# Rope keys in two groups of 64 columns, half of the expert combination as diagonal products, and another load order in the readout

## The chip, the cores and the metric

The kernel runs on one core of a Trainium2 chip. The core has five instruction streams: TensorE (PE in the rows; PEld is its weight load), VectorE (DVE), ScalarE (ACT), GpSimd (POOL) and SyncE (SP), which here only issues transfers. The metric is the device time of one execution in microseconds (us), taken as the median over runs. All arithmetic is in 32-bit floats.

## What is computed

The reference is a chain of three layers over 512 tokens x of 1024 features, with a context of 256 tokens: a gated-delta layer followed by a mixture of 64 experts, an RWKV layer, and a latent-attention (MLA) layer. Three places matter here. Cut to them:

```python
# 1. end of the first layer: six experts per token, weighted, then gate, add, norm
x = x + gt2 * moe_ffn(...)            # sum over the TOP_K = 6 chosen experts
x = rmsnorm(x, g_final)
# 2. readout of the RWKV layer, for all 768 tokens
yf = y[0] + jnp.flip(y[1], 1)
yn = ((yf - mean) * lax.rsqrt(var + GN_EPS)).reshape(B, T, D) * lnx_g + lnx_b
o = (yn + bonus.reshape(B, T, D)) * jax.nn.silu(gate)
d = o @ w_out                         # then x = x + g * d
# 3. inputs of the attention layer
p = h @ w_in
q_c, kv_c, k_pe, gate = jnp.split(p, [Q_LORA, Q_LORA + KV_LORA, Q_LORA + KV_LORA + QK_ROPE], axis=-1)
k_pe = concatenate([x1 * c - x2 * s, x1 * s + x2 * c])   # 32 rope features, x tokens only
```

## The kernel before, in words

The program is a row of phases. Each phase is a block with one instruction stream per engine, written out by hand and kept in that order; engines wait for each other through counted semaphores, and at a phase's end all engines meet at a barrier. Tokens lie in tiles of 128 (P): NT = 6 tiles, JC = 2 of context and JX = 4 of x. D = 1024, KD = 8 blocks of 128 features. Three phases are touched.

**combine** (span time about 1373 to 1431 us). The expert rows of x come back from memory as `rows[:, j, k, :]`, k = 0..5 of token tile j. SP asks for them in eight loads of 1.5 MB (`in0` to `in7`; `in(2j)` holds k = 0..2 of tile j and `in(2j+1)` k = 3..5), all on one queue, then for the context (`ctx_in`). DVE alone does the sum: six passes `acc = row * weight + acc` per tile (L2437), then the gate (L2440), the addition to the tokens (L2442) and, one tile behind, `norm(j-1)` (L2424, L2428). ACT takes the lengths (L2396, L2402) that norm needs, and at the end the squares that the next layer's norm needs; L2418 and L2447 close the phase. PE has no work in it.

**rwkv_readout** (about 2242 to 2381 us). For each of the six tiles j: DVE and ACT make the normed row `y` from two halves that the scan left in memory (`R.mean`, `R.centre`, `R.sum`, `R.finish`), POOL scales the bonus (`R.values`, L3114, L3117), PE turns it (`turn`, L3600), multiplies it with the output weights in two halves (`project`, L3610, 16 products each), and DVE adds the result to the tokens (`add`, L3706 and L3709). Tiles 0 and 1 are normed in the phase before. PE also works off one slice of the next layer's modulation weights per tile (`M.part`, L246; slices are 2 MB, `M.load`). The order on each engine is fixed:

```python
# PE, for j: project(j, 0), turn(j + 1), M.part(j), M.sum(j - 1), project(j, 1)
# DVE, for j: add(j, 0), copy_in(j + 1), norm(j + 2), add(j, 1)
```

`add(0, 0)` first waits for `x_in`, the landing of the tokens `K.X` (3 MB) and of the two gate rows `K.gate` (0.5 MB each). `R.load(sp, j)` is four loads of 0.5 MB (y, y2, bonus, gate) into one of two slots; R.load(j) may start when tile j-2 is turned.

**mla_inputs** (about 2392 to 2506 us). PE makes the latents (L3800, ten units), then the rope keys (L3806), then the gate (L3815, 64 products). The rope keys use a weight block of 96 columns, in which the 32 columns stand at 0 and at 64 (zeros elsewhere, set by POOL), and a second block with the halves exchanged: three passes over columns of `hT` (256 context tokens, 512 x tokens plain, 512 x tokens exchanged), 8 products each. DVE then copies and rotates (L3852 to L3857) and SP copies the result to further partitions.

Of the kernel before, what the change touches and what calls it, by code (L numbers as in the profile page):

```python
# [2363 lines left out]
def combine(K, I, acc, ys, w_of, spare, inv):  # L2364
# [6 lines left out]
    names = ("added gated ctx_in g_in sq_done rms_done v_step normed rms2_done " + " ".join(f"in{n}" for n in range(len(LOADS))))  # L2371
    with ExitStack() as c, phase(nc, names) as (block, S):
        buf = lambda name, shape: c.enter_context(sbuf(nc, name, shape, F32))
        gb, junk, st = buf("gain", [P, D]), buf("junk", [P, D]), buf("stats", [P, 5, NT])
        rows = spare[:, 0:JX * TOP_K * D].rearrange("p (j k n) -> p j k n", j=JX, k=TOP_K)

# [12 lines left out]
        def _(act):  # L2389
# [31 lines left out]
        def _(dve):  # L2421
# [9 lines left out]
            for j in range(JX):  # L2431
                for k in range(TOP_K):
                    if k % (TOP_K // 2) == 0:
                        dve.wait_ge(S[f"in{LOADS.index((j, k // (TOP_K // 2)))}"], 16)
                    if k:
                        dve.wait_ge(S["added"], j * TOP_K + k)
                    dve.scalar_tensor_tensor(out=acc[:, j, :], in0=rows[:, j, k, :], scalar=w_of[:, k, j:j + 1],  # L2437
                                             in1=acc[:, j, :], op0=ALU.mult, op1=ALU.add).then_inc(S["added"], 1)
                dve.wait_ge(S["added"], (j + 1) * TOP_K)
# [1104 lines left out]
def rwkv_readout(K, I, R, tokens, gate_rows):  # L3544
# [6 lines left out]
    with ExitStack() as c, phase(nc, names, R.S) as (block, S):  # L3551
# [219 lines left out]
def mla_inputs(K, I, qc, kvc, ssq, gT, kT, L, ws, pool_):  # L3771
# [4 lines left out]
    names = "rot lat_mm copied squared pe_mm rope1 w_zero pe_out doubled gate_mm gate_out"  # L3776
    with ExitStack() as c, phase(nc, names, L) as (block, S):
        wg, rest = gate_weights(pool_), pool_[:, 2 * KD * 512:]
        wr = rest[:, 0:2 * KD * QK].rearrange("p (a k n) -> p a k n", a=2, k=KD)
        t = rest[:, 2 * KD * QK:2 * KD * QK + 2 * TX].rearrange("p (a n) -> p a n", a=2)  # L3780
# [11 lines left out]
        def _(pe):  # L3792
# [41 lines left out]
        @block.gpsimd  # L3834
        def _(pool):
            pool.memset(wr[:, :, :, :], 0.0).then_inc(S["w_zero"], 1)

        @block.vector
        def _(dve):
            dve.wait_ge(S["w_in"], 16)  # L3840
            dve.wait_ge(S["w_zero"], 1)
# [517 lines left out]
```

## Time and profile before

| | |
|---|---|
| median of 3 runs | 2868.86 us (2866.93 to 2870.2) |
| the profiled execution | 2869.81 us, span 2868.0 us |
| instructions in it | 45580 |
| granted TensorE clock, mean | 0.931 of full speed |
| PE / PEld / DVE / ACT / POOL busy | 86% / 50% / 47% / 25% / 17% of the span |
| moved by DMA | 471.24 MB, mean 164 GB/s |

Busy shares are means over all phases; PE is busy most of the time but idle in some phases. What a change in one phase is worth has to be read from that phase. A matmul of 32-bit floats shows as two rows of the profile per product in the code (64 products at L3815 are 128 rows), so a count "x48" in a row is 24 products.

### The profile page before, as it was taken

Reading aid. Unit: us, or ns where it says so; the run is one execution under the profiler, and the core shown is the slowest. Engines: PE = TensorE matmul, PEld = TensorE weight load, DVE = VectorE, ACT = ScalarE, POOL = GpSimd, SP = SyncE. Lnnn points to the kernel's source line nnn. Section 1 sums busy time; section 2 is a strip of 40 time slices with the busy share of each in tenths; the row PEclk is TensorE's granted clock in tenths of the full one; section 3 lists DMA queues with packets and bytes.
Section 4 is the critical chain, followed back from the end, with each engine's and each line's share of the span. In section 5 each row is a group of like instructions: output and inputs, shape, how many; then the busy total and the mean of one; then the engine's idle time right before and its main releaser. Section 6 shows DMA issues by size and latency. Waiting matters only on the chain. (4 is left out here: it accounts for less than half of the span.)

```text
span 2868.0 us, 45580 instructions
## 1 busy us (share of the span) xinstructions
PE 2465.2 (86%) x18102; PEld 1445.2 (50%) x18102; DVE 1346.4 (47%) x2688; ACT 709.0 (25%) x1273; POOL 487.4 (17%) x474
## 2 busy tenths in 40 slices
PE   4999764987899999998079999979999599989998
PEld 2554354954444443343035557448887346455553
DVE  1550646533611111111678895976666561044442
ACT  3111440102211111111225561123333113044441
POOL 0000142300111111111000000033332230035550
PEclk7999776999899999999589999999999799999999
DMA  6110610014789999996525656334554832021001
GB/s 243 67 59 1 235 23 17 7 59 168 268 333 391 387 418 407 399 388 262 204 87 136 169 153 191 114 121 131 136 164 124 319 118 97 8 42 22 10 30 66
DMA packets 328951, 471.24 MB, mean 164 GB/s; under 512 B 151497, under 2 KB 225139, under 8 KB 304037
## 3 DMA queue, kind: packets, MB, share of 16 engines
q1 hardware_dynamic: 302677, 373.92, 37.9%
q10 hardware_dynamic: 12960, 69.21, 5.9%
q0 software_dynamic: 13104, 25.19, 2.3%
q8 instruction: 146, 2.39, 0.3%
q14 instruction: 64, 0.52, 0.1%
HBM read 413.82 MB, written 76.55 MB: 171 GB/s over the span
## 5 line engine op out<-in xcount | busy, mean ns | idle before, releaser
L1980 PE MATMUL psum<-ex_w,hT 128*64 128x512 f32 (+1 forms) x1104 | 330.6, 619 | 27.4 <-DMA ex_w<-in_exp_w_up 25.7
L1980 PEld LDWEIGHTS psum<-ex_w,hT 128*64 128x64 f32 (+1 forms) x1104 | 125.6, 159 | 226.7 <-issue 224.4
L4126 POOL TENSOR_SCALAR mla_pool<-mla_pool,at_stats 128x768 f32<-128x768 f32 x64 | 140.3, 2206 | 253.1 <-DVE at_stats L4144 253.1
L2212 DVE COPY slot_act_t<-psum 128x256 f32<-128x256 f32 x45 | 19.1, 424 | 327.0 <-PE psum L1988 327.0
L551 PE MATMUL psum<-hT,weights 128*128 128x512 f32 x384 | 166.8, 592 | 0.0
L1996 PE MATMUL psum<-ex_w,slot_act_t 128*64 128x512 f32 (+1 forms) x552 | 163.4, 597 | 1.4 <-DVE slot_act_t L2212 1.4
L1965 POOL DMA_INDIRECT scratch_ys<-slot_out,slot_row x45 | 45.4, 1008 | 468.2 <-issue 405.6
L551 PEld LDWEIGHTS psum<-hT,weights 128*128 128x128 f32 x384 | 73.0, 190 | 86.7 <-issue 86.1
L2168 ACT ACTIVATE slot_silu<-psum 128x256 f32<-128x256 f32 x45 | 17.3, 385 | 400.2 <-PE psum L1980 400.2
L3323 PE MATMUL psum<-rs_r_ident,rs_k_ident 64*64 64x96 f32 x1536 | 86.5, 252 | 15.3 <-POOL rs_k_ident L3295 14.0
L4024 PE MATMUL psum<-mla_kT,at_qT 128*128 128x512 f32 (+1 forms) x256 | 93.3, 489 | 2.6 <-DVE at_qT L4136 1.6
L1996 PEld LDWEIGHTS psum<-ex_w,slot_act_t 128*64 128x64 f32 (+1 forms) x552 | 55.8, 153 | 75.8 <-issue 71.2
L2715 PE MATMUL psum<-rh_lerp,rh_w 128*128 128x512 f32 (+1 forms) x256 | 91.1, 513 | 1.8 <-issue 1.8
L2219 DVE COPY slot_out<-psum 128x512 f32<-128x512 f32 x45 | 31.1, 692 | 128.9 <-PE psum L1996 128.9
L4149 DVE TENSOR_REDUCE at_stats<-psum 128x1 f32<-128x768 f32 x64 | 61.1, 955 | 61.8 <-PE psum L4024 61.6
L4099 ACT ACTIVATE mla_pool<-psum,at_stats 128x768 f32<-128x768 f32 x64 | 57.7, 902 | 127.5 <-DVE at_stats L4154 127.5
L2792 PE MATMUL psum<-rh_w,rh_lerp 128*128 128x256 f32 (+1 forms) x288 | 84.9, 457 | 0.0
L2679 PE MATMUL psum<-rh_lerp,rh_w 128*128 128x512 f32 (+1 forms) x256 | 83.9, 486 | 0.7 <-issue 0.7
L2792 PE MATMUL psum<-tokens,rh_lerp 128*128 128x512 f32 x192 | 82.7, 592 | 0.0
L3323 PEld LDWEIGHTS psum<-rs_r_ident,rs_k_ident 64*64 64x64 f32 x1536 | 67.7, 134 | 25.2 <-POOL rs_k_ident L3295 15.1
L3502 ACT ACTIVATE rs_w<-psum 128x256 f32<-128x256 f32 x96 | 36.9, 384 | 175.5 <-PE psum L3339 175.4
L3454 DVE TENSOR_TENSOR rs_right<-psum,rwkv_decay 64x512 f32<-64x512 f32 x94 | 64.6, 688 | 27.3 <-PE psum L3370 25.8
(612 smaller groups left out, 4731.0 us busy)
## 6 DMA issues: line engine op xcount, KB each, us to landing
ex_w<-in_exp_w_gate SPq DMA_DIRECT2D x64, 1024.0 KB, 9.1
ex_w<-in_exp_w_up SPq DMA_DIRECT2D x64, 1024.0 KB, 18.9
ex_w<-in_exp_w_down ACTq DMA_DIRECT2D x60, 1024.0 KB, 10.2
mod_ring<-in_w_mod SPq DMA_DIRECT2D x12, 2048.0 KB, 14.0
scratch_features<-tokens SPq DMA_DIRECT2D x96, 256.0 KB, 3.7
weights<-in_w_in SPq DMA_DIRECT2D x6, 2048.0 KB, 8.0
ex_w<-in_mod_w SPq DMA_DIRECT2D x6, 2048.0 KB, 12.5
ex_w<-scratch_ys SPq DMA_DIRECT2D x8, 1536.0 KB, 19.0
```

The lines of the kernel that those rows point to most:

```text
L551: mm = pe.matmul(K.bank[2 * (f % 4)][:, :], K.wring[:, n % RING, k, m * P:(m + 1) * P], K.hT[:, k, TC:TT], start=(k == 0), stop=(k == KD - 1))
L1980: mm = pe.matmul(bank[at:at + n, :], XT[:, k, at:at + n], W[:, 0:2, k * DE:(k + 1) * DE], start=(k == 0), stop=(k == KD - 1))
L1996: mm = pe.matmul(bank[at:at + n, :], aT[:, m, at:at + n], W[:, 2, m * D + h * 512:m * D + (h + 1) * 512], start=(m == 0), stop=(m == 1))
L2679: mm = pe.matmul(K.bank[b][:, 0:t1 - t0], rk_w(s)[:, 1, k, :], lerp[:, 0, k, t0:t1], start=(k == 0), stop=(k == KD - 1))
L2715: mm = pe.matmul(K.bank[2 + seg][:, 0:t1 - t0], rk_w(s)[:, 0, k, :], lerp[:, 1, k, t0:t1], start=(k == 0), stop=(k == KD - 1))
L2792: mm = pe.matmul(K.bank[u % 4][:, 0:cols], lerp[:, n, k, j * P:(j + 1) * P], w[:, k, :], start=(k == 0), stop=(k == KD - 1))
L3323: m = pe.matmul(K.bank[scb(u, k)[p]][kb_at[p], ch * P:ch * P + W], KI[part, k, ch, kb_at[p]], RI[part, k, ch, :], start=True, stop=True)
L3454: dve.tensor_tensor(RV[part, u % 2, ch, p::2, :], K.bank[SB][part, :].rearrange("p (k n) -> p k n", n=HD), Dg[part, d, :, at:at + 1].broad ...
L4024: mm = pe.matmul(K.bank[2 * (u % 2) + b][:, 0:t1 - t0], qT[:, s, h, qt * P:(qt + 1) * P], kT[:, s, h, t0:t1], start=True, stop=True)
L4099: act.activation(Pm[:, q % 2, u, :], K.psum[:, b * 512:b * 512 + TT], ACT.Exp, bias=st[:, 1, u:u + 1], scale=SCALE, accum_out=st[:, 2, u:u ...
L4126: pool.tensor_scalar(Pm[:, q % 2, u, :], Pm[:, q % 2, u, :], st[:, 3, u:u + 1], None, ALU.mult)\
L4149: dve.tensor_reduce(st[:, 0, u:u + 1], K.psum[:, b * 512:b * 512 + TT], AX.X, ALU.max)\
```

## The change

Three independent edits. In combine, tiles 1 to 3 sum only the expert rows k = 0..2 on DVE; rows k = 3..5 are summed by PE as products with diagonal matrices that hold the weights (made by ACT from the identity), two halves of 512 columns with three products each, into two PSUM banks, and DVE adds that with one pass. ACT takes the squares of the context after tile 2 and not at the end. In the readout SP asks for tile 2's four arrays right after the vectors, ahead of the first slice of modulation weights, the tokens and the gate rows; it waits first for the scan's stores and for `turned`. The third slice of modulation weights, and those after it, come later in SP's order. In mla_inputs the weight block has 64 columns (32 plain, 32 exchanged); two groups g multiply it with columns 0..383 and 384..767 of `hT`, and write partitions 0..63 and 64..127 of one PSUM bank. POOL's clearing of the block is gone, and DVE's rotation takes its inputs by group.

```diff
@@ combine: names and TensorE @@
-    names = ("added gated ctx_in g_in sq_done rms_done v_step normed rms2_done " + " ".join(f"in{n}" for n in range(len(LOADS))))
+    names = ("diag_set half_mm added gated ctx_in g_in sq_done rms_done v_step normed rms2_done " + " ".join(f"in{n}" for n in range(len(LOADS))))
...
+        HALF = TOP_K // 2
+        diag = buf("weight_diagonals", [P, JX - 1, HALF, P])
+        total = lambda j: K.psum[:, (j % 2) * 2 * 512:(j % 2 + 1) * 2 * 512]
+
+        @block.tensor
+        def _(pe):
+            for j in range(1, JX):
+                pe.wait_ge(S["diag_set"], HALF * j)
+                pe.wait_ge(S[f"in{LOADS.index((j, 1))}"], 16)
+                if j > 2:
+                    pe.wait_ge(S["added"], TOP_K + (j - 2) * (HALF + 1))
+                for n in range(2):
+                    for m in range(HALF):
+                        mm = pe.matmul(total(j)[:, n * 512:(n + 1) * 512], diag[:, j - 1, m, :],
+                                       rows[:, j, HALF + m, n * 512:(n + 1) * 512], start=(m == 0), stop=(m == HALF - 1))
+                mm.then_inc(S["half_mm"], 1)
@@ combine: ScalarE, the diagonals first, the context squares inside the loop @@
+            for j in range(1, JX):
+                for m in range(HALF):
+                    act.activation(diag[:, j - 1, m, :], K.ident, ACT.Copy, scale=w_of[:, HALF + m, j:j + 1])\
+                        .then_inc(S["diag_set"], 1)
             for j in range(JX):
                 lengths(j)
                 if j:
                     next_lengths(j - 1)
-            act.wait_ge(S["ctx_in"], 16)
-            for j in range(JC):
-                square(K.X[:, j, :], st[:, 3, j:j + 1], squares[0])
+                if j == JX - 2:
+                    act.wait_ge(S["ctx_in"], 16)
+                    for n in range(JC):
+                        square(K.X[:, n, :], st[:, 3, n:n + 1], squares[0])
             next_lengths(JX - 1)
@@ combine: VectorE @@
-                for k in range(TOP_K):
+                done = TOP_K + (j - 1) * (HALF + 1) if j else 0
+                for k in range(HALF if j else TOP_K):
...
+                if j:
+                    dve.wait_ge(S["half_mm"], j)
+                    dve.wait_ge(S["added"], done + HALF)
+                    dve.tensor_tensor(acc[:, j, :], acc[:, j, :], total(j), ALU.add).then_inc(S["added"], 1)
@@ rwkv_readout: SyncE @@
             vectors_in(sp, I, vec, S["vec_in"])
+            for b in range(2):
+                sp.wait_ge(S[f"y_st{b}"], 16 * 4 * 2 * NT)
+            sp.wait_ge(S["turned"], 1)
+            R.load(sp, 2)
             M.load(sp, 0)
             sp.dma_start(K.X[:, :, :], tokens.rearrange("(j p) n -> p j n", p=P)).then_inc(S["x_in"], 16)
             for r in range(2):
                 sp.dma_start(K.gate[:, r, :], gate_rows[r].partition_broadcast(P)).then_inc(S["x_in"], 16)
             M.load_bias(sp)
             M.load(sp, 1)
-            M.load(sp, 2)
-            for b in range(2):
-                sp.wait_ge(S[f"y_st{b}"], 16 * 4 * 2 * NT)
-            for j in range(2, NT):
+            for j in range(3, NT):
                 sp.wait_ge(S["turned"], j - 1)
                 R.load(sp, j)
-                if j < 5:
-                    M.load(sp, j + 1)
+                M.load(sp, j - 1)
+            M.load(sp, NT - 1)
@@ mla_inputs: the rope weights and the key products @@
-        wr = rest[:, 0:2 * KD * QK].rearrange("p (a k n) -> p a k n", a=2, k=KD)
...
+        wr = rest[:, 0:KD * 2 * ROPE].rearrange("p (k n) -> p k n", k=KD)
...
-            pe.wait_ge(S["rot"], 1)
-            for b, (n, t0, t1) in enumerate(((0, 0, TC), (0, TC, TT), (1, TC, TT))):
-                for k in range(KD):
-                    mm = pe.matmul(K.bank[2 + b][0:QK, 0:t1 - t0], wr[:, n, k, :], K.hT[:, k, t0:t1],
-                                   start=(k == 0), stop=(k == KD - 1))
+            pe.wait_ge(S["rot"], 3)
+            for k in range(KD):
+                for g in range(2):
+                    mm = pe.matmul(K.bank[2][g * 2 * ROPE:(g + 1) * 2 * ROPE, 0:TT // 2], wr[:, k, :],
+                                   K.hT[:, k, g * TT // 2:(g + 1) * TT // 2], start=(k == 0), stop=(k == KD - 1))
             mm.then_inc(S["pe_mm"], 1)
...
-        @block.gpsimd
-        def _(pool):
-            pool.memset(wr[:, :, :, :], 0.0).then_inc(S["w_zero"], 1)
-
...
-            for at in (NOPE, 0):
-                dve.tensor_copy(wr[:, 0, :, at:at + ROPE], ws[:, :, pe0:pe0 + ROPE])
-                dve.tensor_copy(wr[:, 1, :, at:at + half], ws[:, :, pe0 + half:pe0 + ROPE])
-                ins = dve.tensor_copy(wr[:, 1, :, at + half:at + ROPE], ws[:, :, pe0:pe0 + half])
-            ins.then_inc(S["rot"], 1)
+            dve.tensor_copy(wr[:, :, 0:ROPE], ws[:, :, pe0:pe0 + ROPE]).then_inc(S["rot"], 1)
+            dve.tensor_copy(wr[:, :, ROPE:ROPE + half], ws[:, :, pe0 + half:pe0 + ROPE]).then_inc(S["rot"], 1)
+            dve.tensor_copy(wr[:, :, ROPE + half:2 * ROPE], ws[:, :, pe0:pe0 + half]).then_inc(S["rot"], 1)
             dve.wait_ge(S["pe_mm"], 1)
...
-                dve.tensor_tensor(t[r, 0, :], K.bank[3][r, :], K.cos[h], ALU.mult).then_inc(S["rope1"], 1)
-                dve.tensor_tensor(t[r, 1, :], K.bank[4][r, :], K.sin[h], ALU.mult).then_inc(S["rope1"], 1)
...
+                for g, (c0, c1) in enumerate(x_cols):
+                    xs = slice(x0, x0 + c1 - c0)
+                    dve.tensor_tensor(t[r, 0, xs], K.bank[2][plain[g], c0:c1], K.cos[h][:, xs], ALU.mult)\
+                        .then_inc(S["rope1"], 1)
+                    dve.tensor_tensor(t[r, 1, xs], K.bank[2][turned[g], c0:c1], K.sin[h][:, xs], ALU.mult)\
+                        .then_inc(S["rope1"], 1)
+                    x0 += c1 - c0
```

How the instructions stand on three engines, before and after.

On DVE in combine, one tile's worth as the difference shows it (`hT` is the accumulator acc, `ex_w` the expert rows, `tokens` is K.X):

```order
-L2437 SCALAR_TENSOR_TENSOR hT<-ex_w,w_of,hT 128x1024 x6
-L2440 TENSOR_TENSOR hT<-hT,mod_gate 128x1024
-L2442 TENSOR_TENSOR tokens<-tokens,hT 128x1024
-L2424 RECIPROCAL stats<-stats 128x1
-L2428 SCALAR_TENSOR_TENSOR tokens<-tokens,stats,gain 128x1024
+L2460 SCALAR_TENSOR_TENSOR hT<-ex_w,w_of,hT 128x1024 x3
+L2465 TENSOR_TENSOR hT<-hT,psum 128x1024
+L2467 TENSOR_TENSOR hT<-hT,mod_gate 128x1024
+L2469 TENSOR_TENSOR tokens<-tokens,hT 128x1024
+L2446 RECIPROCAL stats<-stats 128x1
+L2450 SCALAR_TENSOR_TENSOR tokens<-tokens,stats,gain 128x1024
```

Three of six weighted passes are replaced by one addition from PSUM, which stands after them; the rest keeps its order.

On SP in the readout, after the four small vectors, before:

```order
L237 DMA ro_mod_ring<-in_mod_w 128x8x512
L3564 DMA tokens<-scratch_tokens 128x6x1024
L3566 DMA mod_gate<-scratch_gate_rows 128x1024 x2
L230 DMA ro_mod_row<-in_mod_b 2x512 x6
L237 DMA ro_mod_ring<-in_mod_w 128x8x512 x2
L3095 DMA ro_y<-scratch_y 128x1024
L3096 DMA ro_y_1<-scratch_y 128x1024
L3097 DMA ro_bonus<-scratch_rwkv 128x1024
L3098 DMA ro_gate<-scratch_rwkv 128x1024
```

and of the change:

```order
L3122 DMA ro_y<-scratch_y 128x1024
L3123 DMA ro_y_1<-scratch_y 128x1024
L3124 DMA ro_bonus<-scratch_rwkv 128x1024
L3125 DMA ro_gate<-scratch_rwkv 128x1024
L237 DMA ro_mod_ring<-in_mod_w 128x8x512
L3595 DMA tokens<-scratch_tokens 128x6x1024
L3597 DMA mod_gate<-scratch_gate_rows 128x1024 x2
L230 DMA ro_mod_row<-in_mod_b 2x512 x6
L237 DMA ro_mod_ring<-in_mod_w 128x8x512
L3122 DMA rs_a<-scratch_y 128x1024
```

The four loads of tile 2 have moved from behind three slices, the tokens, the gate rows and the biases to the front; the third slice stands behind tile 3's loads.

On PE in mla_inputs (`mla_pool` holds the rope weights and then the gate weights), before:

```order
L3800 MATMUL psum<-ml_w,hT 128x384 x32
L3800 MATMUL psum<-ml_w,hT 128x256 x48
L3806 MATMUL psum<-hT,mla_pool 96x256 x8
L3806 MATMUL psum<-hT,mla_pool 96x512 x16
L3815 MATMUL psum<-hT,mla_pool 128x512 x64
```

and of the change:

```order
L3828 MATMUL psum<-ml_w,hT 128x384 x32
L3828 MATMUL psum<-ml_w,hT 128x256 x48
L3834 MATMUL psum<-hT,mla_pool 64x384 x16
L3843 MATMUL psum<-hT,mla_pool 128x512 x64
```

24 products with 96 columns are replaced by 16 with 64 columns at the same place between the latents and the gate.

## Rows read from the trace of the kernel before

**Rows 1.** The page's first part: busy us, share of the span, rows.

```profile
PE 2465.2 (86%) x18102; PEld 1445.2 (50%) x18102; DVE 1346.4 (47%) x2688; ACT 709.0 (25%) x1273; POOL 487.4 (17%) x474
```

**Rows 2.** Timeline of mla_inputs (start, us, what, [idle before]), and one stage's busy times.

```profile
2402.65 0.49 ACT L3825 ACTIVATE mla_pool<-psum 128x384 f32<-128x384 f32 x1 [4.20 <-PE psum L3800]
2407.81 0.49 ACT L3825 ACTIVATE mla_pool<-psum 128x384 f32<-128x384 f32 x1 [4.20 <-PE psum L3800]
2433.49 17.35 PE L3806 MATMUL psum<-hT,mla_pool 128*96 128x256 f32 x48
2450.60:2505.80 55.20, 55.18 (x129) 24.13 (x127) 6.64 (x12) 4.18 (x7) 0.00 (x0) 1.00 0.03 7
```

**Rows 3.** Timeline: an expert's gate and up products, two column groups in turn.

```profile
1343.18 7.04 PE L1980 MATMUL psum<-ex_w,hT 128*64 128x512 f32 x32
```

**Rows 4.** Timeline of combine, DVE and ACT.

```profile
1389.70 7.95 DVE L2437 SCALAR_TENSOR_TENSOR hT<-ex_w,w_of,hT 128x1024 f32<-128x1024 f32 x6
1397.69 1.22 DVE L2440 TENSOR_TENSOR hT<-hT,mod_gate 128x1024 f32<-128x1024 f32 x1
1401.48 7.95 DVE L2437 SCALAR_TENSOR_TENSOR hT<-ex_w,w_of,hT 128x1024 f32<-128x1024 f32 x6
1421.24 1.22 DVE L2440 TENSOR_TENSOR hT<-hT,mod_gate 128x1024 f32<-128x1024 f32 x1
1425.46 1.28 DVE L2428 SCALAR_TENSOR_TENSOR tokens<-tokens,stats,gain 128x1024 f32<-128x1024 f32 x1
1428.81 1.06 ACT L2396 ACTIVATE junk<-tokens 128x1024 f32<-128x1024 f32 x1
```

**Rows 5.** Loads in2 and in3: issue and landing; then a 2 us stretch (last: DMA share, GB/s).

```profile
L2381 SPq DMA_DIRECT2D ex_w<-scratch_ys x2: 570/574/577, 1374.8 to 1375.5; - x2
DMA to landing us min/median/max: 14.0/15.6/17.2
1401.00:1403.00 2.00, 0.00 (x0) 0.00 (x0) 1.96 (x3) 1.72 (x5) 0.00 (x0) 0.50 1.03 412
```

**Rows 6.** PE after a pause, at two places (in the stretches PEclk stands before DMA).

```profile
1432.16 3.56 PE L479 MATMUL psum<-const,norm_xn 128*128 128x128 f32 x16 [72.52 <-DVE norm_xn L462]
1435.00:1437.00 2.00, 2.00 (x18) 2.00 (x18) 1.98 (x5) 2.00 (x5) 0.00 (x0) 0.88 1.32 223
2248.54 3.75 PE L3610 MATMUL psum<-rs_r_ident,ro_oT 128*128 128x512 f32 x4 [4.44 <-DVE ro_oT L3694]
2250.00:2255.00 5.00, 5.00 (x7) 1.86 (x6) 3.74 (x4) 0.00 (x0) 0.00 (x0) 0.53 1.03 398
2251.23 0.33 PEld L3610 LDWEIGHTS psum<-rs_k_ident,ro_oT 128*128 128x128 f32 x1 [0.52 <-issue]
2252.09 0.33 PEld L3610 LDWEIGHTS psum<-rs_k_ident,ro_oT 128*128 128x128 f32 x1 [0.52 <-issue]
```

**Rows 7.** Groups by line and form: a DVE pass from PSUM (busy us, mean ns).

```profile
L3706 DVE TENSOR_TENSOR rs_y<-psum,mod_gate 128x512 f32<-128x512 f32 x12 | 8.3, 688 | 32.4 <-PE psum L3610 23.3 <-DMA mod_gate<-scratch_gate_rows 9.0
```

**Rows 8.** Timeline of the readout, DVE and PE.

```profile
2262.87 0.69 DVE L3706 TENSOR_TENSOR rs_y<-psum,mod_gate 128x512 f32<-128x512 f32 x1 [9.03 <-DMA mod_gate<-scratch_gate_rows]
...
2264.20 0.68 DVE L3694 COPY ro_oT<-psum 128x512 f32<-128x512 f32 x1
...
2275.61 1.23 DVE L3133 TENSOR_TENSOR ro_y<-ro_y,ro_y 128x1024 f32<-128x1024 f32 x1 [10.72 <-DMA ro_y<-scratch_y]
...
2278.33 2.93 DVE L3140 TENSOR_TENSOR ro_y<-ro_y,ro_stats 128x1024 f32<-128x1024 f32 x1
...
2289.32 1.97 PE L3600 MATMUL psum<-const,ro_y 128*128 128x128 f32 x8 [13.98 <-DVE ro_y L3158]
```

**Rows 9.** Readout's loads: gate rows' issue and landing, and a stretch (last: GB/s).

```profile
L3566 SPq DMA_DIRECT2D mod_gate<-scratch_gate_rows x2: 598/1362/2126, 2245.3 to 2247.5; - x2
DMA to landing us min/median/max: 15.3/15.8/16.3
2255.00:2260.00 5.00, 5.00 (x25) 2.48 (x27) 0.00 (x0) 0.40 (x1) 0.00 (x0) 1.00 1.04 412
```

More of the change, by code:

```diff
@@ L2431, in _ @@
             for j in range(JX):
[L2432 to L2434 removed]
+                done = TOP_K + (j - 1) * (HALF + 1) if j else 0
+                for k in range(HALF if j else TOP_K):
+                    if k % HALF == 0:
+                        dve.wait_ge(S[f"in{LOADS.index((j, k // HALF))}"], 16)
                     if k:
[L2436 removed]
+                        dve.wait_ge(S["added"], done + k)
                     dve.scalar_tensor_tensor(out=acc[:, j, :], in0=rows[:, j, k, :], scalar=w_of[:, k, j:j + 1],
                                              in1=acc[:, j, :], op0=ALU.mult, op1=ALU.add).then_inc(S["added"], 1)
[L2439 removed]
+                if j:
+                    dve.wait_ge(S["half_mm"], j)
+                    dve.wait_ge(S["added"], done + HALF)
+                    dve.tensor_tensor(acc[:, j, :], acc[:, j, :], total(j), ALU.add).then_inc(S["added"], 1)
+                dve.wait_ge(S["added"], TOP_K + j * (HALF + 1))
                 dve.tensor_tensor(acc[:, j, :], acc[:, j, :], gate, ALU.mult).then_inc(S["gated"], 1)
@@ L3775, in mla_inputs @@
     units = [(0, j) for j in range(JC, NT)] + [(1, j) for j in range(NT)]
-    names = "rot lat_mm copied squared pe_mm rope1 w_zero pe_out doubled gate_mm gate_out"
+    names = "rot lat_mm copied squared pe_mm rope1 pe_out doubled gate_mm gate_out"
     with ExitStack() as c, phase(nc, names, L) as (block, S):
         wg, rest = gate_weights(pool_), pool_[:, 2 * KD * 512:]
-        wr = rest[:, 0:2 * KD * QK].rearrange("p (a k n) -> p a k n", a=2, k=KD)
-        t = rest[:, 2 * KD * QK:2 * KD * QK + 2 * TX].rearrange("p (a n) -> p a n", a=2)
+        wr = rest[:, 0:KD * 2 * ROPE].rearrange("p (k n) -> p k n", k=KD)
+        t = rest[:, KD * 2 * ROPE:KD * 2 * ROPE + 2 * TX].rearrange("p (a n) -> p a n", a=2)
         junk = c.enter_context(sbuf(nc, "ml_junk", [P, QL], F32))
@@ L3840, in _ @@
             dve.wait_ge(S["w_in"], 16)
-            dve.wait_ge(S["w_zero"], 1)
             half = ROPE // 2
             pe0 = QL + KVL
-            for at in (NOPE, 0):
-                dve.tensor_copy(wr[:, 0, :, at:at + ROPE], ws[:, :, pe0:pe0 + ROPE])
-                dve.tensor_copy(wr[:, 1, :, at:at + half], ws[:, :, pe0 + half:pe0 + ROPE])
-                ins = dve.tensor_copy(wr[:, 1, :, at + half:at + ROPE], ws[:, :, pe0:pe0 + half])
-            ins.then_inc(S["rot"], 1)
+            dve.tensor_copy(wr[:, :, 0:ROPE], ws[:, :, pe0:pe0 + ROPE]).then_inc(S["rot"], 1)
+            dve.tensor_copy(wr[:, :, ROPE:ROPE + half], ws[:, :, pe0 + half:pe0 + ROPE]).then_inc(S["rot"], 1)
+            dve.tensor_copy(wr[:, :, ROPE + half:2 * ROPE], ws[:, :, pe0:pe0 + half]).then_inc(S["rot"], 1)
             dve.wait_ge(S["pe_mm"], 1)
+            plain, turned = ([slice(g * 2 * ROPE + n * ROPE, g * 2 * ROPE + (n + 1) * ROPE) for g in range(2)] for n in range(2))
+            x_cols = ((TC, TT // 2), (0, TT // 2))
             for h, r in enumerate((slice(NOPE, QK), slice(0, ROPE))):
                 for s in range(2):
-                    dve.tensor_copy(kT[r, s, h, 0:TC], K.bank[2][r, 0:TC]).then_inc(S["pe_out"], 1)
-                dve.tensor_tensor(t[r, 0, :], K.bank[3][r, :], K.cos[h], ALU.mult).then_inc(S["rope1"], 1)
-                dve.tensor_tensor(t[r, 1, :], K.bank[4][r, :], K.sin[h], ALU.mult).then_inc(S["rope1"], 1)
-                dve.wait_ge(S["rope1"], 2 * h + 2)
+                    dve.tensor_copy(kT[r, s, h, 0:TC], K.bank[2][plain[0], 0:TC]).then_inc(S["pe_out"], 1)
+                x0 = 0
+                for g, (c0, c1) in enumerate(x_cols):
[5 more added lines that the diff above has]
+                    x0 += c1 - c0
+                dve.wait_ge(S["rope1"], 4 * h + 4)
                 for s in range(2):
```

## The prediction

> **What bounds the kernel now.** I read the page's busy shares first: PE is busy 86% of the span [rows 1]. So PE sets the time in most phases, but 14% is left in which it waits, and a mean does not say where. Each of the three edits stands in another phase, with barriers between, so I read the timeline of each phase for what ends its waits, and add the three results.
>
> In mla_inputs PE runs without a pause: a latents unit of 8 products over 384 columns follows the last by 5.16 us (2407.81 less 2402.65), the key products take 17.35 us, and the gate products behind them fill 55.18 of 55.20 us, in which DVE has 6.64 us of work [rows 2]. PE is the bound here. In combine DVE goes from pass to pass: six weighted passes take 7.99 us (1397.69 less 1389.70), and from the gate pass to the next tile's first pass it is 3.79 us [rows 4]. Data come at 412 GB/s meanwhile [rows 5], so one load of 1.57 MB lands each 3.8 us and a tile each 7.6; DVE, with 11.8 us per tile, is the bound. In the readout the chain is DVE's: it waits 9.03 us for the gate rows, goes on until it has copied tile 1, waits 10.72 us for tile 2's y, norms tile 2, and only then does PE, idle for 13.98 us, get tile 2 to turn [rows 8].
>
> **Rope keys: 12.0 us less.** 5.16 us for 8 products is 0.645 us for one of 384 columns, so 0.86 for 512 and 0.43 for 256. Before: 16 x 0.86 + 8 x 0.43 = 17.2 us, which the 17.35 (with the last one's drain) confirms [rows 2]. After: 16 products of 384 columns, 10.3 us one after another. But the two groups of a k write partitions 0..63 and 64..127, and so do the two halves of an expert's products: there 16 products of 512 columns took 7.04 us, where one by one they would be 13.8 [rows 3]. The order, k outside and group inside, and the one bank are the same, so I take 5.2 us: 12.0 saved, and 6.9 if nothing overlaps. The weights are the same block for both groups, which that row doesn't have; I see no reason in it for a wait. DVE's rotation gets more and shorter passes, but all of it lies under the gate products. Three DVE copies and POOL's clearing disappear; they ran beside the latents' products, where nobody waited for them.
>
> The Trainium skill, TensorE: Matmul & The Clock Gate, section "Measured speedup vs the span model", gives 2.38x for three column tiles, 0.79 of the ideal. By that two tiles would give 1.6x, the keys 6.5 us, this term 10.7 and the forecast 1.3 us more (an estimate from the page). The expert row shows 1.96x, and the sum goes by the row.
>
> **Combine: 3.3 us less.** DVE drops 3 passes of 1.33 us (4.0) and gets one addition from PSUM of 1024 columns. No row has one that long; a 512-column pass from PSUM is 0.688 [rows 7], twice that is 1.38; one of 1024 without PSUM is 1.22 [rows 4]. I take 1.29 with its gap. If PE were always ready, each of tiles 1 to 3 would end 2.7 us earlier: 8.1 in all.
>
> PE isn't ready for tile 1. Its input in3 was issued at 1375.4 and landed 17.2 later, at 1392.7 (the issue and landing of in2 give 1388.8) [rows 5]. DVE starts the tile at 1389.7 and is through three passes at 1393.7. PE needs six products, after 12 us of idleness or more (the phase has no PE work, and PE was idle 72.52 us when the next one began). At half clock a row of 512 columns takes 0.86 us (2252.09 less 2251.23), a product is two rows, so six are 10.3; at full clock 5.2. How long it stays at 1.2 GHz is read at two places: begun at 1432.16, the mean of 0.88 in 1435 to 1437 puts the rise at 1435.5, after 3.3 us; begun at 2248.54, the 0.53 in 2250 to 2255 puts it at 2254.7, after 6.2 us [rows 6]. Each us at half clock costs half a us: 6.8 to 8.3 us. I take 7.6 and 0.2 for handing over: ready at 1400.5, a new DVE wait of 6.8 us. The gate pass of tile 1 is then at 1401.8, against 1397.69: 4.1 late. Each further tile takes 3.79 + 4.0 + 1.29 = 9.1 where it took 11.8, if PE is ready. For tile 2 PE starts at once when in5 lands (1392.7 + 7.7 = 1400.4), warm, done by 1405.9, wanted at 1409.6. For tile 3 in7 lands at 1408.1; even at half clock PE is done at 1418.4, and it is wanted at 1418.7. So tile 3's gate pass is at 1401.8 + 18.2 = 1420.0, against 1421.24: 1.2 less.
>
> Behind it, the tail: DVE ends tile 3's norm at 1426.7, but ACT takes its square at 1428.81, because two squares of the context stand ahead [rows 4]. They move into the loop, where ACT idles; the context (1 MB more at that rate) has landed by 1411. That gives 2.1. ACT's nine diagonals lie in the wait for the first loads. Sum 3.3.
>
> Bounds: PE cold throughout gives 10.5 us for tile 1 (gate pass at 1404.6), then tile 2 at 1415.1 and tile 3 at 1425.4: 4.2 late, 2.1 late with the tail. PE never waited for gives 8.1 + 2.1 = 10.2 less.
>
> **Readout: 5.0 us less.** Tile 2's four arrays (2.1 MB) go to the head of the queue, which moves 412 GB/s [rows 9]; they need 5.1 us of it, and the 10.72 us wait goes. What is late next is x_in. All in front of it is pushed back by 2.1 MB / 412 GB/s = 5.1 us. The second gate row landed at 2247.5 + 15.3 = 2262.8 [rows 9], where DVE's wait ended; now 2268.1, with 0.2 for SP's wait on `turned`. In DVE's order norm(2) is behind add(0, 0) and copy_in(1), 2.0 us of work (2264.20 + 0.68 less 2262.87), so it starts at 2270.2 instead of 2275.61: 5.4 earlier, and turn(2) with it, 2283.9 instead of 2289.32. PE's project(1, 0) also waits for copy_in(1); before, PE went idle at 2289.32 - 13.98 = 2275.3, now some 2 us later, still 6 us before turn(2). The first weight slice is 5.1 us later too, and PE wants it between project(0, 0) and project(0, 1); a delay there comes out of the same 6 us. After turn(2) the order and the work are as before, and the later slices have a tile's time or more.
>
> I take 5.0 and not 5.4, since POOL's pass over tile 2's bonus waits for the biases, which are as late as the gate rows, and now falls on norm(2)'s first passes; one such DVE pass took 2.93 where its neighbours take 1.23 [rows 8]. The Trainium skill, SBUF — State Buffer, section "Who interferes with whom", makes that a lock: a DVE pass with two SBUF inputs and a POOL instruction that reads SBUF exclude each other for a whole instruction. If it held twice in norm(2), it would cost a further 1.7; the 2.93 agrees with one such hold. Bounds: x_in not pushed back gives 10.7 less (norm(2) at 2264.9); x_in pushed back by twice as much gives nothing.
>
> **Sum.** 12.0 + 3.3 + 5.0 = 20.3 us. The profiled execution took 2869.81 us with a span of 2868.0; 20.3 off is 2849.5. The median is 0.95 lower: 2848.5.
>
> **The rivals.**
> (a) PE is cold or slow in combine: the clock stays at its lower level through the matmuls of tile 1 and falls again in the pauses between tiles. For it: PE works there 5 of 9 us at best. Against: both starts in [rows 6] rose within 6.2 us. Combine +2.1 instead of -3.3: 2853.9. Chance 0.13.
> (b) The two key groups don't overlap: sharing one weight block, or one bank. Only 6.9: 2853.6. Against it is [rows 3]. Chance 0.07.
> (c) The readout gains little: x_in is late by more, because the queue shares out what is outstanding and doesn't serve in order. Then norm(2) starts where it did: 2853.5. Chance 0.15. If it serves so that x_in isn't late, 2843. Chance 0.10.
> (d) Slower than before: the order of loads starves PE. If the first weight slice is late, PE stands in `M.part(0)` with project(0, 1) and project(1, 0) behind it, some 16 us of work ahead of turn(2) (two halves at 16 x 0.43 = 6.9, the slice and a turn). So from 2268 on each us costs one, and from 2288 on all 20.3 are undone. Against it: the slice and what stands ahead of it are 4.2 MB, 10.2 us at 412 GB/s, from about 2246 on. The time would be 2869 to 2878. Chance 0.03.
> (e) The change does less than said in two places at once, 2860 to 2868: 0.05.
> The forecast itself, 2845 to 2852: 0.47.
>
> **How the numbers follow.** 0.2% of 2868.86 is 5.7 us, about what a measurement tells from no change. Cases (a) to (c) all stay faster than that. Range 2841 to 2858: it holds the forecast, (a), (b), (c) and most of combine's good end; outside are (d), (e), and two of the good or of the bad ends together. Faster 0.93, same 0.04, slower 0.03.
>
> **What would show it.** Key products: about 5.3 us for 32 rows in mla_inputs, rows of both groups in pairs. Combine: one wait of DVE for PE of 6 to 7 us ahead of tile 1's addition, none at tiles 2 and 3, the phase 3 us shorter, no context squares at its end. Readout: DVE's first wait ends near 2268 (on the old time axis), no wait for y of tile 2, PE's idle time ahead of turn(2) near 6 to 7 us. Wrong would be: key products near 10 us; a wait at tile 2 or 3; a DVE wait for y that is still there, or a PE wait for a weight slice.

## The result, and the profile after

The changed kernel takes 2845.23 us in the median of 5 runs (2842.52 to 2853.91), the one before 2869.29 in 5 (2866.93 to 2875.64). The ratio is 0.9918, with a 95% interval of 0.9901 to 0.9935. The medians differ by 24.1 us, and the ratio makes it 23.5, where 20.3 were forecast. A second set of runs of the same program gave 2844.51, ratio 0.9922 (0.9907 to 0.9938).

The table has the lengths of the stretches in the traces, in us. A phase starts with the first transfer that SP issues in it, and combine ends with the end of its last reciprocal; the forecast is the change against the kernel before.

| stretch | before | changed | changed, again | forecast |
|---|---|---|---|---|
| combine, first load to last reciprocal | 57.16 | 53.08 | 52.94 | -3.3 |
| combine's end to readout's start | 811.59 | 808.15 | 811.69 | 0 |
| readout's start to its turn(2) | 47.21 | 43.98 | 42.46 | -5.4 |
| readout, whole, to the next phase's load | 139.26 | 134.92 | 134.59 | -5.0 |
| key products to the load behind mla_inputs | 73.90 | 62.06 | 62.06 | -12.0 |
| span | 2868.0 | 2843.4 | 2844.9 | -20.3 |

Timeline of the changed kernel in combine (the DVE lines answer to [rows 4]; L2460 is the weighted pass, L2465 the new addition, L2467 the gate pass):

```profile
1388.71 3.92 DVE L2460 SCALAR_TENSOR_TENSOR hT<-ex_w,w_of,hT 128x1024 f32<-128x1024 f32 x3
...
1391.67 6.90 PE L2390 MATMUL psum<-ex_w,weight_diagonals 128*128 128x512 f32 x12 [33.20 <-DMA ex_w<-scratch_ys]
1398.60 1.22 DVE L2465 TENSOR_TENSOR hT<-hT,psum 128x1024 f32<-128x1024 f32 x1 [5.97 <-PE psum L2390]
1399.35 5.39 PE L2390 MATMUL psum<-ex_w,weight_diagonals 128*128 128x512 f32 x12 [0.78 <-DMA ex_w<-scratch_ys]
1399.86 1.22 DVE L2467 TENSOR_TENSOR hT<-hT,mod_gate 128x1024 f32<-128x1024 f32 x1
...
1407.68 1.22 DVE L2465 TENSOR_TENSOR hT<-hT,psum 128x1024 f32<-128x1024 f32 x1
...
1418.01 1.23 DVE L2467 TENSOR_TENSOR hT<-hT,mod_gate 128x1024 f32<-128x1024 f32 x1
...
1423.55 1.06 ACT L2413 ACTIVATE junk<-tokens 128x1024 f32<-128x1024 f32 x1 [0.48 <-DVE tokens L2450]
```

DVE waits once, 5.97 us at tile 1, for PE, which could begin only when its rows had landed and took 6.90 us; tiles 2 and 3 are not waited for. The last square on ACT starts 0.03 us after DVE's last pass (1422.23 + 1.29) and is what ACT had waited 0.48 us for; no square of the context is ahead of it. PE's work for tile 3 started at the upper clock and fell to the lower one in the middle (granted clock 0.50 from 1409.2 to 1411.7), 7.08 us for the six products; it was done at 1414.06, 2.7 us before DVE wanted it.

Timeline of mla_inputs (it answers to [rows 2]):

```profile
2420.43 5.38 PE L3834 MATMUL psum<-hT,mla_pool 128*64 128x384 f32 x32
...
2425.74 55.20 PE L3843 MATMUL psum<-hT,mla_pool 128*128 128x512 f32 x128
```

and of the readout (to [rows 8]; L3734 and L3737 are add, L3722 the copy of tile 1, L3160 norm(2)'s first pass, L3141 and L3144 GpSimd's passes over tile 2's bonus):

```profile
2259.64 1.25 POOL L259 TENSOR_TENSOR rs_am<-rs_am,ro_mod_row 2x512 f32<-2x512 f32 x1 [25.00 <-DMA ro_mod_row<-in_mod_b]
2259.69 0.69 DVE L3734 TENSOR_TENSOR rs_y<-psum,mod_gate 128x512 f32<-128x512 f32 x1 [14.63 <-DMA mod_gate<-scratch_gate_rows]
2260.41 2.90 DVE L3737 TENSOR_TENSOR tokens<-tokens,rs_y 128x512 f32<-128x512 f32 x1
2260.87 1.90 POOL L3141 TENSOR_TENSOR ro_bonus<-ro_bonus,rwkv_bonus 128x1024 f32<-128x1024 f32 x1
2262.84 2.68 POOL L3144 TENSOR_TENSOR ro_bonus<-ro_bonus,rs_am 128x1024 f32<-128x1024 f32 x1
2263.24 0.68 DVE L3722 COPY ro_oT<-psum 128x512 f32<-128x512 f32 x1
2263.84 2.77 DVE L3160 TENSOR_TENSOR ro_y<-ro_y,ro_y 128x1024 f32<-128x1024 f32 x1
...
2277.39 1.09 PE L3628 MATMUL psum<-const,ro_y 128*128 128x128 f32 x8 [4.00 <-DVE ro_y L3185]
```

The 10.72 us wait for y is gone. The wait for the gate rows has grown from 9.03 to 14.63 us, and two DVE passes that took 0.69 and 1.23 us now take 2.90 and 2.77. Of PE's wait ahead of turn(2), 13.98 us before, 4.00 are left.

### The profile page after: what moved, and what is told of

It is laid out like the page before. It is cut to its first block and busy times, and to the rows that moved or that the text cites. A ratio compares the mean times of both kernels' runs of the same rounds, so it can differ in the third digit from the quotient of the medians.

```text
span 2843.4 us, 45625 instructions
## 1 busy us (share of the span) xinstructions
PE 2474.6 (87%) x18122; PEld 1447.7 (51%) x18122; DVE 1341.0 (47%) x2683; ACT 711.3 (25%) x1282; POOL 484.3 (17%) x473
## 5 line engine op out<-in xcount | busy, mean ns | idle before, releaser
L621 DVE SCALAR_TENSOR_TENSOR conv_out<-conv_in,param_cols_b,conv_out 128x256 f32<-128x256 f32 (+1 forms) x144 | 77.2, 611 | 0.0
```

What stands on the lines that cost most here:

```text
L621: ins = dve.scalar_tensor_tensor(out=dst, in0=src, scalar=wt, in1=dst, op0=ALU.mult, op1=ALU.add)
```

## The experiments

There were twelve runs. The first four tell the terms apart and what two executions of one program differ by.

**Each edit alone, and the whole again.** `keys_only`, `combine_only` and `readout_only` are the kernel before with that part of the diff shown above; `after_again` is the changed kernel unaltered.

> Only the rope keys are changed; combine and readout as in the kernel before. Theory (the terms are those of the prediction, and what the whole change gained beyond them is the drift of the clock's level from one execution to another): 12 us less than before, 2857, and the key products take 5.4 us of trace time. Rival (something in the changed key products also helps what comes later): more than 14 us less. Phases other than mla_inputs should be as before within a few us, in either direction.

> Only combine is changed. Theory: 4 us less than before, 2865; the phase from SP's first load to the last reciprocal takes 53.1 us instead of 57.2, with one DVE wait of about 6 us for PE. Rival (the PE work in combine leaves the clock in another state for the next phases, which is where the unforeseen gain of the whole change came from): 7 to 9 us less, 2861, and the stretch from the end of combine to the start of the readout is some 3.4 us shorter than before in every execution.

> Only SP's order in the readout is changed. Theory: 3 us less than before, 2866 (the wait for y is gone, x_in comes 5.5 us later, and GpSimd's two passes over the bonus hold up two DVE passes by 2.2 and 1.5 us). Rival (the term is 5 or more as forecast, and the difference in the trace is the clock's): 5 to 6 us less, 2864.

> The changed kernel once more, unaltered, to see what two executions of one program differ by. Theory (drift): 2845 again within 3 us, but the stretches outside the three changed places, up to combine and from combine to the readout, differ from the first trace by 1 us or more. Rival (these stretches got shorter through the change): they come out as in the first trace, that is 1.2 and 3.4 us shorter than before.

The medians beside 23 runs of the kernel before (2867.46): keys 2856.15, ratio 0.9966 (0.9954 to 0.9979); combine 2861.01, 0.9977 (0.9968 to 0.9986); readout 2863.28, 0.9985 (0.9976 to 0.9995). By the ratios these are 9.7, 6.6 and 4.3 us, 20.6 together, where the whole gave 22.4 (1 - 0.9922) beside the same 23 runs; by the medians 11.3, 6.5 and 4.2, 22.0 together, and the whole 23.0. The interval of each term is some 3 us to either side, so these times agree with the forecasts of the keys and of the readout, but can't tell 12 from 10 or 5 from 3. For combine the interval is 4.0 to 9.2 us: alone it is worth more than the 3.3 forecast, and its median is that of its rival. In the traces the keys and the readout change their own stretch by what they change it in the whole: key products 62.12 and not 73.90; readout 135.04 whole.

Combine doesn't. Alone it took 54.71 us, 2.5 less than before, where the two traces of the whole have 4.1 and 4.2 less. Seven traces of this study have the same instructions in combine. Two have 53.08 and 52.94; the other five (`combine_only`, `tokens_first`, `biases_early`, `norm_before_add`, `keys_groups_outer`) have 54.71, 54.31, 54.15, 54.45 and 54.11. What differs is DVE's wait for PE at tile 1, 5.97 and 5.86 us in the two and 6.89 to 7.31 in the five, and behind it the length of the stretch at the lower clock. In these rows of the changed kernel the third figure from the end is the granted clock:

```profile
1391.70:1394.70 3.00, 3.00 (x4) 1.45 (x5) 0.93 (x1) 0.00 (x0) 0.00 (x0) 0.50 1.02 407
1395.00:1398.50 3.50, 3.50 (x9) 1.30 (x7) 0.00 (x0) 0.00 (x0) 0.00 (x0) 1.00 1.03 411
```

and of `tokens_first`, with DVE's wait:

```profile
1390.80:1396.30 5.50, 5.50 (x7) 2.38 (x8) 1.04 (x1) 0.00 (x0) 0.00 (x0) 0.50 1.03 412
1399.06 1.22 DVE L2465 TENSOR_TENSOR hT<-hT,psum 128x1024 f32<-128x1024 f32 x1 [7.22 <-PE psum L2390]
```

The stretch from combine's end to the readout was 811.47, 806.96, 810.11 and 811.69 us in these four, 811.59 before. So `combine_only` did show the shorter stretch of its rival, but `after_again`, which has the same edit, did not, and in the eleven traces of this study with an edit of combine it lies between 805.95 and 811.90, 808.8 in the mean; in the three without it is 810.11 to 811.59. The 3.4 us of the first trace are therefore not an effect of the edit that comes in every execution; a tie to it that comes in some is not excluded, and the traces hint at one: the five with the long wait at tile 1 are the five with the shortest stretch behind combine (805.95 to 807.81; all others 808.15 or more). Combine and this stretch together are 860.1 to 861.9 us in those five, 861.23 and 864.63 in the two of the changed kernel, and 867.4 to 869.0 without the edit. No run shows how one brings the other.

**The key groups not beside each other.** On the changed kernel:

```diff
-            for k in range(KD):
-                for g in range(2):
+            for g in range(2):
+                for k in range(KD):
```

> The changed kernel, but the key products run all eight k of group 0 and then all eight of group 1, so that no two neighbours write different halves of the partitions. Same products, same bytes. Theory (half of the keys' gain is that neighbours of the two groups overlap): the 32 rows take 10.3 us instead of 5.3 and the kernel is 5 us slower than the changed one. Rival (the gain is the narrower weight block and fewer columns, in any order): 5.4 us again.

2849.97 us, ratio 0.9927 (0.9909 to 0.9945), which can't be told from the changed kernel's. Timeline of TensorE's weight loads there (start, us, what, count):

```profile
2426.67 0.14 PEld L3834 LDWEIGHTS psum<-hT,mla_pool 128*64 128x64 f32 x1 [0.18 <-issue]
2426.99 0.14 PEld L3834 LDWEIGHTS psum<-hT,mla_pool 128*64 128x64 f32 x1 [0.19 <-issue]
2427.31 0.84 PEld L3834 LDWEIGHTS psum<-hT,mla_pool 128*64 128x64 f32 x7 [0.18 <-issue]
2428.34 0.14 PEld L3834 LDWEIGHTS psum<-hT,mla_pool 128*64 128x64 f32 x1 [0.19 <-issue]
```

and of the changed kernel:

```profile
2423.06 0.14 PEld L3834 LDWEIGHTS psum<-hT,mla_pool 128*64 128x64 f32 x2 [0.18 <-issue]
2423.39 0.14 PEld L3834 LDWEIGHTS psum<-hT,mla_pool 128*64 128x64 f32 x2 [0.18 <-issue]
```

One row per 0.32 us against two. The 32 rows took 9.23 us (10.3 expected) and the stretch from the keys 65.98 us against 62.06, 3.9 more (5 expected). The theory holds but for its size: 7 loads stand in 1.03 us at the border of the groups, where 7 steps would be 2.25, so some rows of group 1 ran beside the last of group 0. The narrower block and the fewer columns are worth 7.9 of the 11.8 us in this order, the side by side 3.9, a third and not the half that was expected.

**The clock at tile 1.** Extra products on PE between the landing of in1 and tile 1's own; they use one diagonal and a bank of their own, and their result is not used.

```diff
+                if j == 1:
+                    pe.wait_ge(S["in1"], 16)
+                    for n in range(14):
+                        pe.matmul(K.psum[:, 2048:2560], diag[:, 0, 0, :], rows[:, 0, n % 6, 0:512], start=True, stop=True)
                 pe.wait_ge(S[f"in{LOADS.index((j, 1))}"], 16)
```

> The changed kernel with 14 more products on PE in combine (their result is not used), between the landing of in1 and tile 1's own products, so that TensorE's clock is at its upper level when in3 lands. It is extra work and says nothing of the output. Theory (tile 1's wait is part half clock, part late data): the six products of tile 1 take 5.2 us instead of 6.9, DVE's wait for PE shrinks from 6.0 to about 4.3 us, and the phase from first load to last reciprocal takes 51.4 instead of 53.0. Rival (the wait is the product's own length at any clock, or the extra products are still running when in3 lands): the phase takes 53 us or more.

A miss by a slip of mine, and the second half of the rival: 14 products are 28 rows, 14.7 us, and ran past the landing. DVE's wait was 9.69 us, the phase 56.73, the kernel 2853.23 (0.9949, 0.9933 to 0.9966). With `range(7)`:

> As combine_warm, with 7 extra products instead of 14 (14 ran on for 5 us after in3 had landed, and made the phase longer). Their result is not used. Theory: they end just before in3 lands, tile 1's six products take 5.2 to 5.4 us instead of 6.9, DVE waits some 4.4 us for PE instead of 6.0, and the phase from first load to last reciprocal takes 51.4 us instead of 53.0. Rival (clock is no part of that wait): 53 again.

Its timeline:

```profile
1382.95 8.58 PE L2388 MATMUL psum<-ex_w,weight_diagonals 128*128 128x512 f32 x14 [23.90 <-DMA ex_w<-scratch_ys]
...
1392.25 5.42 PE L2394 MATMUL psum<-ex_w,weight_diagonals 128*128 128x512 f32 x12 [0.72 <-DMA ex_w<-scratch_ys]
1397.70 1.22 DVE L2469 TENSOR_TENSOR hT<-hT,psum 128x1024 f32<-128x1024 f32 x1 [4.39 <-PE psum L2394]
```

5.42 us instead of 6.90, the wait 4.39 instead of 5.97, the phase 51.95 instead of 53.0. The lower clock was 1.5 us of the wait in the trace shown (in the five traces with the long wait, 2.5 to 2.9); the rest is that PE can't begin before its rows land and then needs 5.4 us. The phase gained 0.5 us less than the wait, since the clock now fell during tile 2 (7.08 us for its products), and DVE waited 0.47 us for PE there. In the kernel's time (2845.43, 0.9908, 0.9890 to 0.9926) 1 us can't be told.

**PE's rows first.** For tiles 1 to 3 SP asks for rows 3..5 ahead of rows 0..2.

```diff
+        ASKED = LOADS[:2] + [(j, 1 - h) for j, h in LOADS[2:]]
...
-            for n, (j, h) in enumerate(LOADS):
+            for n, (j, h) in enumerate(ASKED):
...
-                    .then_inc(S[f"in{n}"], 16)
+                    .then_inc(S[f"in{LOADS.index((j, h))}"], 16)
```

> The changed kernel, but for tiles 1 to 3 SP asks for the rows that PE needs ahead of those that DVE needs. Theory: PE starts tile 1 when the first of the two loads lands, 3.8 us earlier; it is done about when DVE has made its three passes, which now start later (second load at 1391.5 on the changed kernel's axis, so passes end at 1395.6); DVE's wait for PE nearly goes, a data wait of about 2.9 us takes its place, and tile 1's gate pass comes about 2 to 3 us earlier: the phase takes 50 to 51 us instead of 53. Rival (the data set the phase anyway): no gain, since the last load lands at the same time and DVE's passes then stand behind it.

The theory, nearly to the row (DVE's data wait was 2.58 us, 2.9 expected): the phase took 50.02 us.

```profile
1388.84 6.82 PE L2391 MATMUL psum<-ex_w,weight_diagonals 128*128 128x512 f32 x12 [29.31 <-DMA ex_w<-scratch_ys]
...
1392.57 3.93 DVE L2461 SCALAR_TENSOR_TENSOR hT<-ex_w,w_of,hT 128x1024 f32<-128x1024 f32 x3 [2.58 <-DMA ex_w<-scratch_ys]
...
1396.60 1.22 DVE L2466 TENSOR_TENSOR hT<-hT,psum 128x1024 f32<-128x1024 f32 x1
```

PE's products are no faster than in the changed kernel (6.82 us), but nobody waits for them. The kernel took 2841.88, 0.9898 (0.9881 to 0.9915).

**The tokens first, in the readout.** On the changed kernel, tile 2's arrays (with SP's waits for them) behind the biases, but still ahead of the second weight slice:

```diff
-            sp.wait_ge(S["turned"], 1)
-            R.load(sp, 2)
             M.load(sp, 0)
...
             M.load_bias(sp)
+            sp.wait_ge(S["turned"], 1)
+            R.load(sp, 2)
             M.load(sp, 1)
```

> The changed kernel, but in the readout tile 2's four arrays are asked for right behind the first weight slice, the tokens, the gate rows and the biases, and not ahead of them. Theory (x_in pushed back by 5.5 us is what is left of the wait): DVE's first wait ends some 5.3 us earlier, y of tile 2 lands shortly after, and from the readout's start to turn(2) it is 38 us instead of 42.5 to 44. Rival (y is late again and is waited for): 42 or more.

To turn(2) 37.71 us; 2840.21, 0.9896 (0.9879 to 0.9912).

```profile
2254.39 0.69 DVE L3734 TENSOR_TENSOR rs_y<-psum,mod_gate 128x512 f32<-128x512 f32 x1 [9.89 <-DMA mod_gate<-scratch_gate_rows]
...
2256.90 1.23 DVE L3160 TENSOR_TENSOR ro_y<-ro_y,ro_y 128x1024 f32<-128x1024 f32 x1 [0.40 <-DMA ro_y<-scratch_y]
```

This kernel started the readout at 2232.88, so the gate rows' wait ended 21.5 us in; in the changed kernel, which started at 2233.41, 26.3. That is 4.8 of the 6.3 us that turn(2) came earlier; the rest is that only one DVE pass is long here (L3167, 2.91 us, beside GpSimd's first pass over the bonus), less a wait of 0.40 us for y. The readout as a whole took 129.77 us, 5.2 less than in the changed kernel.

**The biases early.** `M.load_bias(sp)` moved to right behind `R.load(sp, 2)`.

> The changed kernel, but in the readout SP asks for the six small bias rows right behind tile 2's arrays and not behind the gate rows. GpSimd waits for them ahead of its two passes over tile 2's bonus. Theory (these passes held up two DVE passes by 2.2 and 1.5 us, which is why this term came out smaller than forecast): GpSimd is done with them before DVE's wait for x_in ends, the DVE passes take 0.7 and 1.2 us again, and from the readout's start to turn(2) it is 40.3 us instead of 44.0. Rival (these long passes have to do with the arriving loads, not with GpSimd): 43 or more, with a long DVE pass still there.

To turn(2) 39.96 us, forecast 40.3; 2842.17, 0.9904 (0.9888 to 0.9921).

```profile
2250.51 1.90 POOL L3141 TENSOR_TENSOR ro_bonus<-ro_bonus,rwkv_bonus 128x1024 f32<-128x1024 f32 x1
2252.49 2.35 POOL L3144 TENSOR_TENSOR ro_bonus<-ro_bonus,rs_am 128x1024 f32<-128x1024 f32 x1
2255.91 0.69 DVE L3734 TENSOR_TENSOR rs_y<-psum,mod_gate 128x512 f32<-128x512 f32 x1 [14.23 <-DMA mod_gate<-scratch_gate_rows]
2256.64 0.69 DVE L3737 TENSOR_TENSOR tokens<-tokens,rs_y 128x512 f32<-128x512 f32 x1
...
2257.85 1.22 DVE L3160 TENSOR_TENSOR ro_y<-ro_y,ro_y 128x1024 f32<-128x1024 f32 x1
```

Both long passes are short again, with x_in as late as before (26.0 us in, against 26.3), so the rival is out: the loads still arrive, and only GpSimd's passes have moved.

**norm(2) ahead of add(0, 0).** With the biases early as well:

```diff
-                add(j, 0)
+                if j:
+                    add(j, 0)
...
                     norm(j + 2)
+                if j == 0:
+                    add(j, 0)
                 add(j, 1)
```

> The changed kernel, but on DVE norm(2) stands ahead of add(0, 0), and SP asks for the biases right behind tile 2's arrays. Theory (after the change DVE stands idle for x_in with tile 2's data already there): norm(2) runs from the copy of tile 1 on, and PE turns tile 2 right after project(1, 0) with hardly a pause: from the readout's start to turn(2) it is 33 us instead of 42.5 to 44, 9 to 11 us less in all. Rival (another wait takes its place: the bonus on GpSimd, or a weight slice that PE needs): 38 us or more.

31.98 us to turn(2), of which the biases early have 4.0 and the new order on DVE 8.0, and 2833.95, 0.9872 (0.9855 to 0.9889). The readout as a whole took 121.78 us, 13.1 less than in the changed kernel; from the next phase's first load to its key products it was then 53.85 us and not 52.10, for a reason that no run shows. PE goes from project(1, 0) to turn(2) without a pause in its line of the timeline:

```profile
2264.44 1.88 PE L3638 MATMUL psum<-rs_inverse,ro_oT 128*128 128x512 f32 x4
...
2266.16 1.04 PE L3628 MATMUL psum<-const,ro_y 128*128 128x128 f32 x8
```

**Both together.** `both` has this and PE's rows first.

> combine_half_first and norm_before_add together, the best that the runs point to. Theory (the phases are apart and the gains add): combine 50.0 to 51.5 us, the readout up to turn(2) 32 us, 2831 in all. Rival (they don't add, since the earlier one only moves the clock's level): 2834 or more.

2829.88 us, 0.9865 (0.9848 to 0.9881), beside 2870.52 for the kernel before: 38.8 us less by the ratio (40.6 by the medians), with combine at 49.97 and the way to turn(2) at 31.67. It beats both kernels of this case.

## Why the prediction was right

**Rope keys.** Forecast 12.0, measured 11.84 in the trace. The order of the groups matters as said, by 3.9 us. Case (b) is out. The products took 5.31 us from the first to the gate's first (2425.74 less 2420.43), full overlap. The estimate of 6.5 us, worked out from the Trainium skill, TensorE: Matmul & The Clock Gate, section "Measured speedup vs the span model", is not what this trace shows.

**Combine.** Forecast 3.3, measured 4.1 and 4.2 in the two traces of the changed kernel, and 2.5 to 3.1 in the five others with the same instructions. The mechanism was right in all seven; that their mean, 3.2, comes so near the forecast is luck in part. The parts in the trace shown: PE at tile 1 forecast 7.6 us, took 6.9; DVE's wait 6.8, was 6.0; the gate pass of tile 1 forecast 4.1 late, was 3.35 late against the first load (27.68 us behind it, before 24.33); the addition forecast 1.29 with its gap, was 1.26; the tail 2.1, was 2.0. The miss is the length of the stretch at half clock, which I read from two places at 3.3 and 6.2 us: six products in 6.90 us with 5.42 at the upper level (the warm run) make it 3.0; in the five others it was 5.0 to 5.8. So both readings come, and the 7.6 us that I took between them stand for neither; why an execution gets one or the other stays open. Case (a) did not come: PE was at its upper level again for tile 2 (5.39 us). The second half of it, that the clock falls in the pauses, came at tile 3 and cost nothing there.

**Readout.** Forecast 5.0, measured 4.3 and 4.7 over the phase, but only 3.2 at turn(2) in the trace shown (4.75 in the second). Over the seven traces with this order of loads it is 3.1 to 4.7 for the phase and 3.0 to 4.75 at turn(2), so the term was forecast too high in all of them. The phase gained 1.1 us more than turn(2) in the trace shown, since turn(2) itself and what follows it took 90.94 us and not 92.05; turn(2) ran in 1.09 us, at the upper clock, where it had taken 1.97. In the second trace it took 1.97 again, and the rest 92.13. The mechanism was right: y's wait gone, x_in what is late next, by 5.5 us (5.3 forecast; 4.65 in the second trace), y never waited for. The term that was mis-sized is "I take 5.0 and not 5.4", the 0.4 us for GpSimd's passes over the bonus. They cost 2.2 + 1.5 us in the trace shown, and before one pass already carried 1.7 [rows 8], so 2.0 more; `biases_early` took 4.0 us away by moving them, 3.7 of it from the two passes and 0.3 from x_in. The rule that I named for this, and whose two holds I did not put into the sum, the lock in the Trainium skill, SBUF — State Buffer, "Who interferes with whom", fits: L3737 ended at 2263.31 and L3160 at 2266.61, each about the length of its own work after a GpSimd instruction's end (2262.77 and 2265.52). The step that failed is that I counted what would collide behind norm(2)'s start only, not the second instruction of add(0, 0) ahead of it: that one is long (2.1 to 3.1 us) in six of the seven traces. In the second trace of the changed kernel it is not (0.69), and GpSimd holds up norm(2)'s first pass alone for longer (3.55 us) and L3162 by 0.8, 3.1 us in all.

PE's part was read wrong too, at no cost. I had it go idle some 2 us later than before and 6 us ahead of turn(2). But copy_in(1) stands behind the long pass of add(0, 0), PE waited 5.00 us for it and began project(1, 0) at half clock (3.75 us for four rows that took 1.88 before), and 4.00 us were left (6.09 in the second trace). So DVE still set the time, and the error did not show.

**The sum.** The three terms are 11.84 + 4.08 + 4.34 = 20.3 us of the trace. That this is the forecast to the tenth is luck: combine came out 0.8 higher, the readout 0.7 lower. The first trace is 24.6 shorter; the other 4.3 lie outside, 1.2 ahead of combine and 3.4 between combine and the readout, less 0.3 elsewhere. The 1.2 is no gain of the change: combine starts at 1369.8 to 1373.4 us in the three traces without its edit. By the ratios of the single edits the change is worth 20.6, by its own 22.4 and 23.5, each give or take some 4 to 5 us. So the forecast fits what the edits do to their own stretches, and what the medians have beyond it is not accounted for.

Of the rivals (c) and (d) can be judged too: x_in was not later than in order, and the first weight slice was not waited for.

## What to carry to other kernels

When a load is moved to the head of a queue, name the next thing in that queue that somebody waits for: here the move turned a 10.7 us wait into 5.5 us more of another, and by the traces putting the tokens first (5.2 us off the readout), or the consumer's work ahead of the wait, gave more than the move had (4.3). When work is handed to an idle engine, give it its input first and count a start at half clock, with a range and not a middle value. Where GpSimd works on SBUF, put it into DVE's waits and not beside DVE's passes over SBUF.

## What the runs showed of the hardware

- Products of two column groups run beside each other in full when they alternate: 32 rows of 384 columns in 5.31 us, two per 0.32 us. Even with the groups one behind the other, some rows at their border overlapped (9.23 us for the 32 instead of 10.3, which is three steps of 0.32).
- A tiny DVE instruction can be held for long: L3162 works on 128x16 and takes 0.17 us alone, 2.69 beside a GpSimd pass, from the run with norm(2) first:

```profile
2253.21 1.26 POOL L259 TENSOR_TENSOR rs_am<-rs_am,ro_mod_row 2x512 f32<-2x512 f32 x1 [17.79 <-ACT rs_am L254]
2253.68 2.69 DVE L3162 TENSOR_SCALAR ro_stats<-ro_stats 128x16 f32<-128x16 f32 x1
...
2254.43 1.90 POOL L3141 TENSOR_TENSOR ro_bonus<-ro_bonus,rwkv_bonus 128x1024 f32<-128x1024 f32 x1
```

  It starts while GpSimd's L259 is running, and ends where the next one, L3141, ends (2256.37 and 2256.33), although that one's record starts 0.75 us after DVE's own: GpSimd's two instructions stand without a gap, and DVE gets its turn behind both. It is the same in the trace shown above, where L3737 starts at 2260.41, inside L259 (2259.64 to 2260.89), and L3141 follows at 2260.87. Not every DVE instruction is held: beside L3144 the copy from PSUM (L3722, 0.68 us in the changed kernel) and the reduction (L3161, 1.22 us in its second trace) took their usual time.
- The stretch of some 810 us between combine and the readout, the same instructions in every kernel here, differed by 6 us between the traces (805.95 to 811.90), and by 3.5 between two of one program (808.15 and 811.69). What it depends on stays open; for edits of a few us the trace's own stretches are a better measure than the total.
- After 33 us of idle time PE was at the lower clock for 3.0 us in two executions of tile 1's products in combine and for 5.0 to 5.8 us in five others, with the same instructions up to there. That moved the phase by 1.0 to 1.8 us.
